# Prompt attention by residue: 25 score tiles a head in place of 37, and what the tiles hand on to each other

## What is computed

```python
def dilated_prompt(q, k, v, window, dilation):
    L = S // dilation
    to_res = lambda t: t.reshape(B, L, dilation, H, D).transpose(0, 2, 1, 3, 4).reshape(B * dilation, L, H, D)
    o, lse = band_attn(to_res(q), to_res(k), to_res(v), window // dilation)
def merge_groups(outs, lses):
    a = jax.nn.softmax(jnp.stack(lses, 0), axis=0)
    return jnp.einsum('gbsh,gbshd->bshd', a.astype(o.dtype), jnp.stack(outs, 0))
```

## Time and profile before

| | |
|---|---|
| time, median of 3 runs | 1779.81 us (1779.38 to 1781.79) |
| span of the profiled execution | 1779.2 us, at a mean granted clock of 0.988 |
| `attend_sample`, last DVE copy of it | 1068.75 us, 0.39 long |
| `attend_prompt` | 1070.2 to 1254.9 us: 184.7 us |
| `finish`, first product | 1255.98 us |

### The profile page before, as it was taken

How to read it: one execution, slowest core, us unless ns; L and a number is a source line. 1 busy time by engine, 2 the same in 40 slices (tenths; PEclk the granted TensorE clock), 3 DMA queues, 4 the chain that set the end, 5 groups by cost and what they waited for, 6 DMA issues and landing times. The chain is left out here.

```text
span 1779.2 us, 32332 instructions
## 1 busy us (share of the span) xinstructions
PE 1710.8 (96%) x10749; PEld 1529.3 (86%) x10749; DVE 1086.7 (61%) x2480; ACT 956.5 (54%) x1649; POOL 868.4 (49%) x496
## 2 busy tenths in 40 slices
PE   6999999999889999999999977898999999999998
PEld 5888888899889999899899956888998989899897
DVE  6747556422388888888888877888444514234251
ACT  5444344432368887888888877988314313122230
POOL 1615233300338878778788747775233433333332
PEclk9999999999999999999999998999999999999999
DMA  7386585645889999999999976320645566666662
GB/s 238 106 290 216 202 300 183 207 132 137 253 308 365 344 351 350 353 347 336 355 360 349 316 232 163 91 73 25 215 146 214 235 259 236 259 236 260 236 259 77
DMA packets 191563, 427.76 MB, mean 240 GB/s; under 512 B 22761, under 2 KB 86122, under 8 KB 190002
## 3 DMA queue, kind: packets, MB, share of 16 engines
q1 hardware_dynamic: 187474, 415.29, 66.8%
q10 hardware_dynamic: 2560, 8.39, 1.6%
q0 software_dynamic: 1376, 2.10, 0.5%
HBM read 392.36 MB, written 120.64 MB: 288 GB/s over the span
## 5 line engine op out<-in xcount | busy, mean ns | idle before, releaser
L1086 POOL TENSOR_TENSOR vv_lo<-v_raw,vv_hi 128x1024 fp32r<-128x1024 f32 x178 | 401.4, 2261 | 147.9 <-ACT vv_hi L1175 145.7
L1986 POOL TENSOR_TENSOR w_lo<-w_raw,w_hi 128x2048 fp32r<-128x2048 f32 x39 | 180.1, 4619 | 318.4 <-ACT w_hi L2000 318.4
L1167 ACT ACTIVATE kt_hi<-ktp 128x1024 fp32r<-128x1024 f32 (+1 forms) x192 | 186.2, 970 | 94.0 <-PE ktp L1351 93.2
L1191 DVE TENSOR_TENSOR kt_lo<-ktp,kt_hi 128x1024 fp32r<-128x1024 f32 (+1 forms) x192 | 220.9, 1151 | 8.1 <-ACT kt_hi L1167 6.2
L1365 PE MATMUL s_ps<-kt_hi,q_st 128*128 128x256 f32 (+3 forms) x768 | 205.9, 302 | 0.8 <-DVE mx_parts L1241 0.4
L1351 PE MATMUL ktp<-ident,k_raw 128*128 128x128 f32 x1440 | 192.0, 276 | 8.3 <-DVEq L1182 3.8
L1351 PEld LDWEIGHTS ktp<-ident,k_raw 128*128 128x128 f32 x1440 | 168.6, 142 | 32.7 <-issue 5.6
L707 PE MATMUL acc<-w_hi,xn_hi 128*128 128x512 f32 x480 | 192.4, 401 | 2.4 <-POOL w_lo L340 2.4
L1175 ACT ACTIVATE vv_hi<-v_raw 128x1024 fp32r<-128x1024 f32 (+1 forms) x192 | 191.4, 997 | 6.2 <-PE o_ps L1381 5.7
L1365 PE MATMUL s_ps<-kt_lo,q_st 128*128 128x256 f32 (+3 forms) x768 | 191.0, 282 | 0.0
L707 PE MATMUL acc<-w_lo,xn_hi 128*128 128x512 f32 x480 | 187.7, 391 | 0.0
(11 more groups left out here) (244 smaller groups left out, 4139.4 us busy)
## 6 DMA issues: line engine op xcount, KB each, us to landing
k_raw<-in_cache_fox_k SPq DMA_DIRECT2D x256, 256.0 KB, 4.9
v_raw<-in_cache_fox_v SPq DMA_DIRECT2D x256, 256.0 KB, 4.6
out_win_kv_sample<-in_cache_win_kv SPq DMA_DIRECT2D x32, 2040.0 KB, 9.5
w_raw<-in_w_in SPq DMA_DIRECT2D x32, 1024.0 KB, 5.9
k_raw<-in_cache_win_kv SPq DMA_DIRECT2D x40, 512.0 KB, 9.5
v_raw<-in_cache_win_kv SPq DMA_DIRECT2D x40, 512.0 KB, 8.6
w_raw<-in_w_up SPq DMA_DIRECT2D x16, 1024.0 KB, 5.3
w_raw<-in_w_down SPq DMA_DIRECT2D x16, 1024.0 KB, 5.1
```

Of the source, the lines that this page charges most:

```text
L1086: gp.tensor_tensor(vv_lo[:, slot, 0:tiles, :], v_raw[:, i % RAW_RING, 0:tiles, :], vv_hi[:, slot, 0:tiles, :].bitcast(F32), ALU.subtract). ...
L1167: act.activation(kt_hi[:, slot, :, 0:n], ktp[:, i % 2, :, 0:n], ACT.Copy).then_inc(k_hi, 1)
L1191: ve.tensor_tensor(kt_lo[:, slot, :, 0:n], ktp[:, i % 2, :, 0:n], kt_hi[:, slot, :, 0:n].bitcast(F32), ALU.subtract).then_inc(k_lo, 1)
L1986: gp.tensor_tensor(w_lo[slot][:], w_raw[:, slot, :], w_hi[slot][:].bitcast(F32), ALU.subtract).then_inc(slab_lo_done, 1)
```

## The change

- The projection stores queries and keys of sets 2 and 3 by residue: token 4m + r goes to column 128 r + m. The stores of four prompt tiles are one transfer, the sample's columns go to arrays of their own (`qn_s`, `kn_s`).
- `attend_prompt` runs over 8 heads x 7 steps. A step is a group of units: SPREAD (sets 2 and 3 of one residue: one tile of 128 x 128 each, side by side, two residues a step), NEAR (set 1, two query tiles a step), FAR (set 0: query tile 3, tile 2, tiles 0 and 1). 8 + 7 + 10 = 25 tiles a head.
- Scores contract over the 64 rows of the head alone; the zero halves are gone.
- `keep` writes the negated scores and takes a minimum, which serves as the bias of the exponential; the separate maximum is gone. Each unit has an exponential and a row sum of its own (12 a head, not 8).
- Probabilities are not normalised. Three outputs a head (SPREAD, NEAR, FAR) are copied out of PSUM, and POOL multiplies them by shares, once a pair. A share is a number per query. NEAR's row minima and sums lie by token, SPREAD's by residue: NEAR's go to DRAM (`send_near`, one 4-byte element at a time) and come back by residue (`take_near`), the shares are worked out in 9 small instructions on DVE, POOL and ACT, go to DRAM (`send_shares`, `send_far`) and come back broadcast over 64 rows (`take_shares`).
- The first pair's queries and keys are loaded and split inside the last sequence of `attend_sample`; masks and the first two heads' bias are loaded there too. Later pairs are split one set a step by ACT and POOL.
- The transposed tiles have 2 PSUM banks, the scores 3, the outputs 3.

```diff
+GROUPS = ((SPREAD, (0, 1)), (SPREAD, (2, 3)), (NEAR, (2, 3)), (NEAR, (0, 1)), (FAR, (3,)), (FAR, (2,)), (FAR, (0, 1)))
+SPREAD_JOBS, NEAR_JOBS, FAR_JOBS = ((0,), (1,), (2, 3)), ((0, 2), (1, 3)), ((0, 1), (2, 3))
+SPREAD_BEHIND, NEAR_BEHIND, FAR_BEHIND = (6, 7, 9), (10, 11), (12, 13)
+KEEP_BEHIND, EXP_P_BEHIND, TURN_BEHIND, LOW_BEHIND = 1, 2, 4, 5
+PART_AT, V_RING = 4, 6
+V_AT = (12, 13, 17, 18)
+FIRST_V_AT = (2, 3, 4, 5)
...
 # attend_sample
-            load_query_half(sp, a, qk_raw, pair_in, 0, 0)
-            load_pair_keys(sp, a, qk_raw, pair_in, 0)
-            load_query_half(sp, a, qk_raw, pair_in, 0, 1)
+            straight(DEC_BATCH, PER_BATCH, ..., (1, first_pair), (7, first_masks))        # SP: 2 MB raw, masks, bias
+            straight(DEC_BATCH, PER_BATCH, ..., (6, first_pair))                          # ACT: 8 copies of 128x512
+            straight(DEC_BATCH, PER_BATCH, ..., (8, first_pair))                          # DVE: 8 subtractions of 128x512
...
 # attend_prompt
+            straight(HEADS, STEPS, (0, raw_ahead), (6, values_ahead), (6, send_near), (7, take_near), (8, bias_ahead),
+                     (10, send_far), (17, send_shares), (18, take_shares))                # SP
+            sp.wait_ge(v_lo_done, SETS * PAIRS)
             load_branch_slab(sp, a, w_raw, slab_loaded, 1)
...
+            def take_near(h, i):
+                if i == 0:
+                    sp.wait_ge(near_sent, 16 * (h + 1))
+                    after(sp, shares_done, h + 1 - STATS)
+                    sp.dma_start(near_stat[:, h % STATS], a["stat_s"][h].rearrange("c (m r) -> m c r", r=RESIDUES)).then_inc(near_in, 16)
...
+            def scale(h, i):                                                              # POOL, at 20, odd heads
+                gp.wait_ge(share_in, 16 * (h + 1))
+                gp.tensor_tensor(x, x, share[:, 2, :], ALU.mult)
+                gp.tensor_tensor(near, near, share[:, 1, :], ALU.mult).then_inc(scaled_apart, 1)
+                gp.tensor_tensor(near, near, x, ALU.add)
+                gp.tensor_tensor(far, far, share[:, 0, :], ALU.mult).then_inc(scaled, 1)
...
+            def score(h, i):
+                after(pe, kept, at - S_BANKS + 1)
+                            last = pe.matmul(s_ps[:, at % S_BANKS, out], q[p % 2][rows_of(h), mine, s, n * P:(n + 1) * P], k[p % 2][rows_of(h), theirs, s, keys], start=(m == 0), stop=(m == 2))
+            def turn(h, i):
+                pe.wait_ge(exp_done, at + 1)
+                after(pe, turned_lo, at - T_BANKS + 1)
```

More of the change, by code:

```diff
@@ L1399 @@
[L1399 to L1425 removed]
+SPREAD, NEAR, FAR = 0, 1, 2
@@ new lines, with raw_cols, unit_tiles, group_cols @@
+PART_ORDER = (2, 3, 1, 0)
+PARTS = 2 * SETS
+PART_AT, V_RING = 4, 6
+V_AT = (12, 13, 17, 18)
+FIRST_V_AT = (2, 3, 4, 5)
+SMALL_ROOM = 4 * P * (4 + 2 * FOX_TILES)
+def raw_cols(ahead, n, s):
+    return ahead["raw"][:, n, s * SEQ:(s + 1) * SEQ]
+def unit_tiles(kind, n):
+    if kind == SPREAD:
+        return [(s, n) for s in range(NATURAL_SETS, SETS)]
+    return [(kind, kt) for kt in range(max(0, n - 1) if kind == NEAR else 0, n + 1)]
+def group_cols(i):
+    kind, units = GROUPS[i]
+    return sum(len(unit_tiles(kind, n)) for n in units) * P
@@ L1427, in attend_prompt @@
+def attend_prompt(nc, a, sem, ident, o_t, ahead, o_all, w_raw, slab_loaded, lead):
     with ExitStack() as ctx:
@@ L1542, in _ @@
+        block = ctx.enter_context(nc.Block())
         @block.sync
@@ L1713, in split_lead, with exponentials @@
-            def split_lead(p, i):
-                if p < PAIRS - 1 or i < CHUNKS - 1:
+            def exponentials(h, i):
+                kind, units = GROUPS[i]
+                act.wait_ge(kept, STEPS * h + i + 1)
+                if kind == FAR:
+                    after(act, far_inverted, h + 1 - STATS)
+                for n in units:
+                    x, (least_of, sum_of) = probs[:, prob_cols(i, n)], (stat[:, h % STATS, kind, c, n:n + 1] for c in range(2))
+                    last = act.activation(x, x, ACT.Exp, scale=-1.0, bias=least_of, accum_out=sum_of)
+                last.then_inc(exp_done, 1)
@@ new lines, in turns_hi @@
+            def turns_hi(h, i):
+                kind = GROUPS[i][0]
+                jobs = len((SPREAD_JOBS, NEAR_JOBS, FAR_JOBS)[kind])
+                after(act, weighed[kind], jobs * h - (1 if kind == SPREAD and i == 0 else 0))
+                act.wait_ge(turned, STEPS * h + i + 1)
+                for cols, places in turned_parts(i):
+                    last = act.activation(pt_hi[:, places, :], t_ps[:, (STEPS * h + i) % T_BANKS, cols].rearrange("p (k n) -> p k n", n=P), ACT.Copy)
+                last.then_inc(turned_hi, 1)
@@ new lines, in values_hi, with stage @@
+            def values_hi(w, first):
+                def stage(h, i):
+                    p = 0 if first else h // 2 + 1
+                    if i == 0 and h % 2 == 0 and p < PAIRS and not (first and h):
+                        act.wait_ge(v_in, 16 * SETS * (p + 1))
+                        old_pair, old = divmod(SETS * p + w - V_RING, SETS)
+                        if old_pair >= 0:
+                            kind = (SPREAD, SPREAD, NEAR, FAR)[old]
+                            act.wait_ge(weighed[kind], len((SPREAD_JOBS, NEAR_JOBS, FAR_JOBS)[kind]) * 2 * (old_pair + 1))
+                        act.activation(v_hi[:, v_slot(p, w)], v_raw[:, w], ACT.Copy).then_inc(v_hi_done, 1)
+                return (FIRST_V_AT if first else V_AT)[w], stage
```

791 lines of the change are left out of this document (405 added, 386 removed).

## The result

The changed kernel takes 1860.3 us (median of 4; 1860.0 to 1860.5) against 1780.2 us before, a ratio of 1.044 with an interval of 1.043 to 1.046: 80 us slower, where I had forecast 11 us faster.

A forecast was written before the change was run, and what follows sets the result against it. PE was taken to bound the kernel, busy 96%, with small waits between in-order engines. Scores -23.6, sample attention +5.5, tail +6, `finish` +1.5 gave -10.6 us: 1769 us, forecast range 1762 to 1776 (chance 0.43), wider range 1754 to 1786.

The forecast's parts named there:

- 29.6 a pair ... 3.5 us ... I leave 3: `attend_prompt`, steady part: 29.6 us PE work, 3.5 for row changes, 3 of waits: 36.1 us a pair, 2.58 a step.
- change of rows: PE in `attend_prompt`: going from 64 to 128 rows and back costs 0.25 us, in each of 14 steps a pair.
- the stretch of the scores with its start: `attend_prompt`, stage start to last score: 7 us plus 53.5 steps of 2.58, 145.0 us for 168.6, difference -23.6.
- Rival B: Waits in `attend_prompt` go: 2.36 to 2.45 us a step, lumps half hidden, -25 us, 1755; chance 0.22.
- the lump: First pair's 8 ACT copies and 8 DVE subtractions in the last sequence of `attend_sample`: +5.5 us, between +2 and +10.
- the tail: Behind the last score: the last head's shares travel through DRAM and back, 22 us for 16.0, +6 us.
- Rival D: Single-element transfer lands in more than 20 us, not 5: tail grows by 15 and more, 1785 and more; chance 0.13.
- costs nothing: Shares' path through DRAM in the steady part of `attend_prompt`: 15 steps of room, some 38 us, so no cost.
- The start of `finish`: PE idle for 13 us before `finish`, which then starts at the lower clock level: +1.5 us.
- ACT, DVE and POOL cover their new work: `attend_prompt`: their edits lie under PE and ACT and cost nothing; ACT near 30 us a pair, POOL 27.
- 5.6 us: `attend_prompt` before the change: waits and handing on, from a pair's 42.7 us less 37.1 of PE work.

The follow-up runs named there:

- g1_best64: f1_best2 with each score product contracting over its own head's 64 rows only: 1843.5 us (1.034 of the kernel before).
- f1_best2: Changed kernel, full result: zero-padded 128-row scores, statistics turned on VectorE and stored in runs of 32, lead split late, loads and first splits moved: 1748.8 us (0.982).
- c2_packed128: Changed kernel with 128-row score products (sum over both heads) and single-element stores made runs of four: 1765.6 us (0.991 of the kernel before).
- f3_all: c2_packed128 with the first pair's splits at the start of `attend_prompt` and the lead split behind the last exponential of the gaps: 1750.8 us (0.983).
- c1_packed: Changed kernel, still 64 rows, with its single-element stores made runs of four elements: 1858.0 us (1.042 of the kernel before).
- c3_later_takes: Changed kernel with 128-row scores and single-element stores, the reads and work behind the stores asked for later, four statistics places: 1836.1 us (1.031).
- c5_wide64: Changed kernel with stores in runs of four; NEAR and FAR scores on 64 rows, SPREAD on 128: 1791.7 us (1.005), ten executions from 1775.1 to 1799.4.
- c4_spread64: Changed kernel with stores in runs of four; SPREAD's scores on 64 rows, NEAR and FAR on 128: 1771.9 us (0.995 of the kernel before).
- f2_warm64: c1_packed with the first pair's scores over 128 rows, all later ones over 64: 1772.0, 1836.1, 1838.8 and 1843.1 us in four executions.
- g2_best_single: f1_best2 with NEAR statistics and FAR's inverted sums again stored one element at a time: 1821.0 us (1.023 of the kernel before).

## Why the prediction was wrong

**The step that failed: "29.6 a pair ... 3.5 us ... I leave 3".** Every duration in it is from rows at clock 1.00, and nowhere did I ask whether the new mix of products would run at it. I weighed the 64-row contraction by its change of rows alone (0.25 us; 0.18 measured) and by its load (as long with either: the shortest of 64 rows takes 183 ns, of 128 rows 187 ns). I took from the earlier trace rows, where 0.70 stands for 5 us after a gap, that only a gap lowers the clock. Here PE had none at 1189 us. What the runs showed in its place: with 64 rows in this mix the granted clock is 0.50 for nearly all of the stage, and the 384-column products start 0.32 us apart, not 0.17. The pair took 55.3 us for 36.1, the stretch of the scores with its start 221.8 for 145.0; the one edit to 128 rows in the mended kernel is worth 95 us (g1_best64 against f1_best2).

The Trainium skill (TensorE: Matmul & The Clock Gate, Part 1: The HAM clock gate) has the clock go by how busy PE has been, and a busy stretch bring it to full. These runs do not agree as far as "busy" is the busy time of the profile: PE is busy 20.00 of 20.00 us at 0.50 with 64-row scores, and 19.25 at 1.00 with 128. The measurement decides.

**At full clock the step was too dear, not too cheap.** With 128 rows and packed stores a pair takes 30.6 us: the 29.6 of my sum and 1.0 more, where I had added 3.5 for the rows and 3 for waits. Rival B's belief that the waits go was right, but its 1755 us are not met by the kernel that it was about: with both causes away c2_packed128 takes 1765.6, since the lump and the tail cost more than B gave them. That f3_all (1750.8) and f1_best2 (1748.8) lie near 1755 is in part luck, as they are without the lump as well.

**Rival D had the right transfer and the wrong way for it to cost.** I gave the store of single elements 5 us to land (10 above), D asked for more than 20, and it took 9.8, from its issue to that of the read behind it (1295.78 to 1305.54 us in the changed kernel's last head). The Trainium skill (DMA: Bandwidth & Descriptors, Rules for kernel authors) warns of one descriptor an element for it; the runs agree: the page of the changed kernel counts 43,441 packets under 512 bytes and that of c1_packed 34,225, and the difference of 9,216 is that of 8 x 1536 single elements to 8 x 384 runs of four. The waits are up to 10.8 us for the one and 4.1 for the other. But I priced it in the tail and wrote that in the steady part the same path "costs nothing", with 15 steps of room, and that SyncE's wait is harmless below 30 us. It has two such waits a head, not one. They follow each other on one queue, with POOL's, ACT's and the next loads' places behind them: 17.7 us a head measured, where a head should take 18 or less. That this makes it a limit of throughput and not a latency with slack is my reading of the waits; c3_later_takes, meant to tell them apart, does not. What is shown is the cost: D was to end at 1785 and more, and the stores alone make 1821 to 1825.

**The lump in the sample attention** was priced 5.5 us, 2 to 10; measured +9.7 us for the stage, and 10.0 us for the whole kernel when it moves. The 2 MB of early loads cost at most 1.8 us of it (496.1 us without the lump but with them, 494.3 before).

**The tail** was priced +6; measured +15.8, of which 11.3 remain with packed stores and full clock. c1_packed shows that the stores were not its main part. What was missing in my chain is ACT's order: `split_lead`, 5 us in one piece, stands ahead of the last head's exponential of the gaps (4.9 us back when it goes behind).

**The start of `finish`** (+1.5) came out at +1.0. That ACT, DVE and POOL cover their new work was right: in c2_packed128, from one copy to the same copy a pair later (1111.2 to 1141.8 us), PE is busy all of 30.6 us, ACT 27.9, DVE 22.0 and POOL 20.6. Two readings of mine were off without touching the sum: ACT's groups of the earlier trace rows and their like add up to 46 us a pair and not 44, and PE stood idle for only 3.9 of the 42.7 us, so not all of the "5.6 us" were waits.

What stays open is what in the 64-row work decides on the clock. Ninety-six rows keep it up, an eighth of 64-row products too, half of them gives either; the same edit leaves the kernel before at full clock after 50 us and this one at the lower level but for some 6 us. It is not the number of changes between 64 and 128 rows: the kernel before has 16 a head there and this one 7. Numbers of rows between 64 and 96 were not tried, nor wider 64-row products in all steps; c5_wide64 has them only beside SPREAD's 128 rows.

## What to carry to other kernels

A price list of durations holds only at the clock it was read at: when a change makes PE's products smaller in rows, look at the granted clock of the stretch first, and let rows of zeros stay where they keep it up. When a store goes element by element, count the waits behind it on its issuing queue and multiply by how often they come round; turn the data first (0.21 us on VectorE here) and store runs. When two limits lie close together, taking one away shows little (2 us here) or exposes the next (35 of 95 us): put both edits and each alone side by side. And look into the one odd window of a long uniform stretch: the 6 us at full clock in the changed kernel's own profile already said that the clock can fall without a gap.

## What the runs showed of the hardware that I had not expected

- PE full and at 1.2 GHz for nearly all of 220 us, 64-row scores in the mix; at 2.4 GHz with 128 rows and otherwise the same instructions (f1_best2 from 1090 us to its last score). With half of the scores on 64 rows the clock falls and comes back once a head, PE being full throughout (c4_spread64).
- One and the same program (f2_warm64) took 1772 us once and 1836 to 1843 us three times; another (c5_wide64) spread over 24 us. The kernel before spreads over 6 in 15 executions.
- A store of 1024 single elements, 4 KB, keeps SyncE waiting for up to 10.8 us (17.4 in g2_best_single); four stores of 8 x 32 elements each, behind a transposition of 0.21 us, for 3.1 us at most.
